# Three blocks of a transformer on one core: new order of the mixer heads, norms on four columns, divided weight tiles in the attention slots

## What is computed

```python
for i in range(2):
    x = x + 0.5 * swiglu(rmsnorm(x), w_gate, w_up, w_down)
    h = rmsnorm(x) @ w_in
    y_mla  = attention(rmsnorm(h_q) @ w_qb, rmsnorm(h_kv) @ w_kvb, rope(h_kpe))   # 8 heads
    y_conv = silu(layernorm(depthwise_conv31(a * sigmoid(g))))                   # 31 taps, 256 channels
    y_hy   = x2 * longconv(x1 * longconv(v))                                     # two rounds, in frequencies
    x = x + concat(rmsnorm(y_mla), rmsnorm(y_conv), rmsnorm(y_hy)) @ w_out
    x = x + 0.5 * swiglu(rmsnorm(x), ...)
x = rmsnorm(x)
proj = rmsnorm(x) @ w_in_2            # state-space branch, and 3 groups of windowed attention, 4 heads each
x = x + (gate_a * ssm(proj) @ w1 + gate_b * attention(proj) @ w2) @ w3
x = x + swiglu(rmsnorm(x), ...)
out = rmsnorm(x)
```

## Time and profile before

| what | us |
|---|---|
| median of 3 runs (lowest, highest) | 3437.59 (3435.35, 3446.17) |
| device time of the profiled execution | 3437.45 |
| its span, first to last instruction | 3435.6 |
| PE busy in it | 3296.0 |
| DVE, ACT, POOL busy | 1797.7, 750.0, 1831.1 |
| mean granted TensorE clock, as a share of full speed | 0.989 |

### The profile page before, as it was taken

How to read it: one execution, slowest core, us unless ns; L and a number is a source line. 1 busy time by engine, 2 the same in 40 slices (tenths; PEclk the granted TensorE clock), 3 DMA queues, 4 the chain that set the end, 5 groups by cost and what they waited for, 6 DMA issues and landing times.

```text
span 3435.6 us, 43891 instructions
## 1 busy us (share of the span) xinstructions
PE 3296.0 (96%) x14456; PEld 2576.4 (75%) x14456; DVE 1797.7 (52%) x1995; ACT 750.0 (22%) x1265; POOL 1831.1 (53%) x1026
## 2 busy tenths in 40 slices
PE   6999999989999999999989999999999999999997
PEld 5888875468887788876457888787777777878885
DVE  6642168663312753138755331476768886753313
ACT  2110115522211111013532220111122322222201
POOL 4556651056666646663026666554455555666664
PEclk9999999999999999999999999999999999999998
DMA  4223230023233322231002323322121222223232
GB/s 138 80 80 98 92 105 19 8 79 96 94 97 97 111 74 86 93 110 61 13 31 92 97 93 97 108 79 68 61 90 62 74 70 72 92 92 98 93 96 73
DMA packets 77141, 280.98 MB, mean 82 GB/s; under 512 B 9350, under 2 KB 9734, under 8 KB 76360
## 3 DMA queue, kind: packets, MB, share of 16 engines
q1 hardware_dynamic: 74016, 268.84, 24.3%
q10 hardware_dynamic: 2984, 10.27, 0.9%
HBM read 276.97 MB, written 2.10 MB: 81 GB/s over the span
## 4 chain that ended last, share of the span: by engine, by line
PE 83%; DVE 11%; issue 3%; ACT 2%; DVEq 0%; ACTq 0%; DMA 0%; SPq 0%
PE bank L499 25%; PE bank L504 24%; PE bank L503 24%; DVE x_lo L1638 1%; PE bank L716 1%; PE bank L780 1%; PE bank L634 1%; PE bank L798 1%; PE bank L704 1%; DVE scaled L1990 1%; DVE square_sum L1648 1%; DVE xbc L2155 0%; DVE y L1878 0%; PE bank L611 0%; PE bank L619 0%
## 5 line engine op out<-in xcount | busy, mean ns | idle before, releaser
L445 POOL TENSOR_SCALAR w_hi<-raw 128x1024 fp32r<-128x1024 f32 x504 | 550.7, 1093 | 1525.1 <-PE bank L499 1518.0
L448 POOL TENSOR_TENSOR w_lo<-raw,w_hi 128x1024 fp32r<-128x1024 f32 x504 | 1267.6, 2515 | 42.1
L499 PE MATMUL bank<-x_hi,w_hi 128*128 128x512 f32 x2896 | 1151.4, 398 | 56.2 <-DVE x_lo L1638 31.4
L504 PE MATMUL bank<-x_hi,w_lo 128*128 128x512 f32 x2896 | 1133.3, 391 | 0.0
L503 PE MATMUL bank<-x_lo,w_hi 128*128 128x512 f32 x2896 | 1132.9, 391 | 0.0
L499 PEld LDWEIGHTS bank<-x_hi,w_hi 128*128 128x128 f32 x2896 | 547.4, 189 | 193.9 <-issue 79.1
L503 PEld LDWEIGHTS bank<-x_lo,w_hi 128*128 128x128 f32 x2896 | 548.0, 189 | 116.2 <-issue 5.3
L504 PEld LDWEIGHTS bank<-x_hi,w_lo 128*128 128x128 f32 x2896 | 546.9, 189 | 116.4
L504 PE MATMUL bank<-hidden_hi,w_lo 128*128 (+1 forms) x880 | 347.6, 395 | 0.0
L499 PE MATMUL bank<-hidden_hi,w_hi 128*128 (+1 forms) x880 | 347.6, 395 | 0.0
L503 PE MATMUL bank<-hidden_lo,w_hi 128*128 (+1 forms) x880 | 347.6, 395 | 0.0
(11 more groups left out here) (372 smaller groups left out, 3260.4 us busy)
## 6 DMA issues: line engine op xcount, KB each, us to landing
raw<-in_w SPq DMA_DIRECT2D x504, 512.0 KB, 3.5
dft<-in_dft ACTq DMA_DIRECT2D x2, 1536.0 KB, 6.8
x<-in_x SPq DMA_DIRECT2D x2, 1024.0 KB, 6.8
out<-x SPq DMA_DIRECT2D x4, 512.0 KB, 2.6
mask<-in_mask ACTq DMA_DIRECT2D x1, 1536.0 KB, 7.1
filt_cos<-in_dft_filter ACTq DMA_DIRECT2D x2, 512.0 KB, 5.5
filt_sin<-in_dft_filter ACTq DMA_DIRECT2D x2, 512.0 KB, 7.3
sel<-in_sel ACTq DMA_DIRECT2D x1, 768.0 KB, 5.5
```

What stands on the lines that cost most here:

```text
L445: nc.gpsimd.tensor_scalar(w_hi[:, s % 2, :], raw[:, s, :], 1.0, 0.0, ALU.mult, ALU.add).then_inc(w_rounded, 1)
L448: nc.gpsimd.tensor_tensor(w_lo[:, s % 2, :], raw[:, s, :], w_hi[:, s % 2, :].bitcast(F32), ALU.subtract).then_inc(w_split, 1)
L499: first = nc.tensor.matmul(out, hi_w, hi, start=start, stop=False)
L504: return nc.tensor.matmul(out, lo_w, hi, start=False, stop=stop)
```

## The change

In the mixer's in-projection the two latent norms are made on four columns: four matmuls that put one column for each 128 tokens into the sum's bank, a root and a reciprocal of 128x4, and four matmuls that spread the columns over a bank again. The second sum and both spreads stand inside a tile, after 2 of its 8 chunks. Ten of the 62 taps, all of accumulator 0, move from the heads into the in-projection on VectorE. In the heads both `inverse` of the first round stand in head 2, the fillers are cut from 28 to 13 for each layer, the fourth score of head 3 comes after its last turn, ScalarE copies a turned tile ahead of the exponential of the same number in the second half of a head, and the first two exponentials of head 0 come ahead of the value copies, behind a small Exp on one column. `spectrum_terms` makes 6 operations instead of 8. In the second block the fourth tile is whole and the second sum behind it, and the waits for the joined norm stand in slot 0 before bank 2. In the slots the third tile beside is divided around the rounds r=2 and r=3; in slot 3 the tile that followed the slot is divided into four pieces and put into bank 0. The negation of the row maximum is made by the reduction itself, and `shift(2)` comes before the value tile. The last norm is made on four columns and the last `x_hi` and `x_lo` are left out, which nobody read. The core of the diff:

```diff
-            def in_projection(tiles, between):
+            def in_projection(tiles, inside, between):
 
                 for n in range(tiles):
                     pe.wait_ge(tile_free, c.next(tile_free))
-                    project(bank[RING[n % len(RING)]][:], arriving=2 if n == 0 else 0).then_inc(tile_ready, 1)
+                    to = bank[RING[n % len(RING)]][:]
+                    if n in inside:
+                        s = take()
+                        project_part(to, s, 0, 2)
+                        inside[n]()
+                        project_part(to, s, 2, DC).then_inc(tile_ready, 1)
+                    else:
+                        project(to, arriving=2 if n == 0 else 0).then_inc(tile_ready, 1)
...
-                    after(mixed_copied, 3)
...
                 for pair in range(2):
                     product(bank[KEY_BANKS[pair]][:], s, 4 + pair, latent_hi[2], latent_lo[2], True, True
                             ).then_inc(k_ready, 1)
+                if g:
+                    after(mixed_copied, 3)
                 query_tile(ROPE_BANKS[1], s, 6, rope_ready)
...
-                if h < 7:
+                if h < 7 and h != 3:
                     scores(h + 1, 3)
                 mix(h, 0)
                 turn(h, 2)
                 mix(h, 1)
                 turn(h, 3)
+                if h == 3:
+                    scores(h + 1, 3)
                 second_unit()
                 mix(h, 2)
-                run_idle({0: 4, 2: 2, 4: 4}.get(h, 0))
                 mix(h, 3)
...
+                def latent_sums(n):
                     if n == 2:
-
-                        after(norm_rms, 1)
+                        after(latent_scaled, 1)
                     after(norm_summed, n)
-                    nc.tensor.matmul(bank[SUM_BANK][:], ones[:], (square_sum[:] if n > 1 else square[:, 0, :]),
-                                     start=True, stop=True).then_inc(norm_sum, 1)
-
-                in_projection(IN_BLOCKS, {1: sum_squares, 4: lambda: latent_norm(1), 6: lambda: latent_norm(2)})
+                    for t in range(TT):
+                        last = nc.tensor.matmul(bank[SUM_BANK][:, t:t + 1],
+                                                (square_sum if n > 1 else square[:, 0])[:, t * P:(t + 1) * P],
+                                                ones[:, 0:1], start=True, stop=True)
+                    last.then_inc(norm_sum, 1)
+
+                def latent_spreads(n):
+                    after(latent_inverted, n)
+                    for t in range(TT):
+                        last = nc.tensor.matmul(bank[SUM_BANK][:, t * P:(t + 1) * P],
+                                                latent_root[:, t:t + 1].broadcast_to([P, P]), ident[:],
+                                                start=True, stop=True)
+                    last.then_inc(latent_spread, 1)
+
+                in_projection(IN_BLOCKS, {5: lambda: latent_spreads(1), 7: lambda: latent_sums(2),
+                                          8: lambda: latent_spreads(2)},
+                              {1: sum_squares, 4: lambda: latent_sums(1)})
+                after(latent_scaled, 2)
...
-                def first_inverse(o, n):
-                    run_idle(n)
-                    inverse(o, 0)
-
-                head(1, nothing, lambda: first_inverse(0, 5))
-                head(2, lambda: inverse(0, 1), nothing)
+                head(1, lambda: run_idle(1), nothing)
+                head(2, lambda: inverse(0, 0), lambda: inverse(0, 1))
                 head(3, lambda: signal_transposes(1), lambda: frequencies(1, 0))
                 head(4, lambda: frequencies(1, 1), nothing)
-                head(5, nothing, lambda: first_inverse(1, 4))
+
+                def first_inverse():
+                    run_idle(2)
+                    inverse(1, 0)
+
+                head(5, lambda: run_idle(1), first_inverse)
                 head(6, lambda: inverse(1, 1), conv_mean)
...
+                    if j == 0 and n == min(FIRST_SUM_BANKS):
+                        pe.wait_ge(both_means, 1)
+                        pe.wait_ge(rms_ready, 3 * LAYERS + 1)
...
+                def spread_tile(first, end):
+
+                    if first == 0:
+                        if more:
+                            pe.wait_ge(vt_ready, c.at(vt_ready) + 2)
+                        split_slot.append(take())
+                    last = project_part(bank[VALUE_TILE_BANK if more else LATE_TILE_BANK][:], split_slot[0], first, end)
+                    if end == DC:
+                        last.then_inc(tile_ready, 1)
+
+                split_slot = []
                 for r in range(RES):
+                    if r == 3 and not more:
+                        spread_tile(2, 4)
...
-                        beside(2)
+                        spread_tile(0, 6 if more else 2)
+                    elif r == 3:
+                        spread_tile(6 if more else 4, DC if more else 6)
...
+                if not more:
+                    spread_tile(6, DC)
...
-                s = take()
-                project_part(bank[VALUE_TILE_BANK][:], s, 0, 2)
+                project(bank[VALUE_TILE_BANK][:]).then_inc(tile_ready, 1)
                 sum_squares(FIRST_SUM_BANKS[1])
-                project_part(bank[VALUE_TILE_BANK][:], s, 2, DC).then_inc(tile_ready, 1)
-
-                pe.wait_ge(both_means, 1)
-                pe.wait_ge(rms_ready, 3 * LAYERS + 1)
                 for j in range(4):
                     attention_slot(j)
-                proj_tile()
...
+            pe.wait_ge(x_summed, c.next(x_summed, DC))
+            for t in range(TT):
+                last = nc.tensor.matmul(bank[SUM_BANK][:, t:t + 1], square_sum[:, t * P:(t + 1) * P], ones[:, 0:1],
+                                        start=True, stop=True)
+            last.then_inc(sum_ready, 1)
+            pe.wait_ge(root_inverted, c.next(root_inverted))
+            for t in range(TT):
+                last = nc.tensor.matmul(bank[SUM_BANK][:, t * P:(t + 1) * P],
+                                        final_root[:, t:t + 1].broadcast_to([P, P]), ident[:], start=True, stop=True)
+            last.then_inc(root_spread, 1)
...
+                        if g == 0:
+                            exponential(0, t)
...
-                        for t in range(3):
+                        for t in range(2):
                             exponential(h + 1, t)
                         turned(h, 2)
+                        exponential(h + 1, 2)
+                        turned(h, 3)
                         exponential(h + 1, 3)
-                        turned(h, 3)
                         return
...
                     for t in range(2, TT):
+                        turned(h, t)
                         exponential(h + 1, t)
-                        turned(h, t)
...
+                nc.scalar.activation(exp_warm[:], eps[:], ACT.Exp)
                 mla_inputs(0)
-                for t in range(TT):
+                for t in range(2, TT):
...
+                early = 10
+                tap_order = [(0, j) for j in range(early)]
+                for j in range(TAPS):
+                    tap_order.append((1, j))
+                    if early + j < TAPS:
+                        tap_order.append((0, early + j))
                 taken, tap_at = [0], [None, None]
...
+                latent_inverse()
+                gate_tiles()
+                latent_scale((2,), KV_NORM)
+                gate_product(0)
+                norm_squares(2, lambda: long_taps(2))
+                long_taps(2)
+                latent_inverse()
+                long_taps(3)
+                latent_scale((0, 1), Q_NORM)
+                dve.sem_inc(latent_ready, 1)
+                gate_tiles()
+                long_taps(3)
+                gate_product(1)
...
-                    nc.vector.tensor_tensor(first[0], re, f_re, ALU.mult)
-                    nc.vector.tensor_tensor(first[1], im, f_im, ALU.mult)
+                    nc.vector.tensor_tensor(products[:, 0:2, :].rearrange("p a n -> p (a n)"), low,
+                                            spectrum[:, k, o, :], ALU.mult)
                     nc.vector.tensor_tensor(first[2], re, f_im, ALU.mult)
                     nc.vector.tensor_tensor(first[3], im, f_re, ALU.mult)
                     (im, re), (f_re, f_im) = halves(high), halves(spectrum[:, 2 + k, o, :])
-                    nc.vector.tensor_tensor(second[0], im, f_re, ALU.mult)
-                    nc.vector.tensor_tensor(second[1], re, f_im, ALU.mult)
+                    nc.vector.tensor_tensor(key_rope[:], high, spectrum[:, 2 + k, o, :], ALU.mult)
...
-                    link(nc.vector.reduce_max(soft_max[:, r % 2:r % 2 + 1], w, AX_X))
-                    link(nc.vector.tensor_scalar(soft_shift[:, r % 2:r % 2 + 1], soft_max[:, r % 2:r % 2 + 1],
-                                                 -1.0, None, ALU.mult), soft_shifted)
```

(1 more changed line is left out.)

159 lines of the change are left out of this document (86 added, 73 removed).

## The result

| | us, median (lowest to highest) | ratio to before, 95% interval |
|---|---|---|
| before | 3440.98 (3435.35 to 3446.17) | |
| changed kernel | 3419.78 (3414.05 to 3422.53) | 0.9939, 0.9926 to 0.9952 |

The change is worth 21 us of the 44 that were forecast; 3419.78 lies outside the stated range of 3382 to 3413. The profiled execution of the changed kernel took 3421.57 us (span 3419.8), so that the two profiles differ by only 15.9 us. Ratios are set against runs of the kernel before on the same chip in the same session.

The account below looks back on a forecast made before the run. TensorE was taken as the main bound (83% of the chain, VectorE 11%), alternating with VectorE in the heads. 2 × (−2) + 2 × (−12.5) − 10.2 − 5.1 = −44.3 from 3437.45 gave 3393.1 us, range 3382 to 3413.

Parts of the forecast that it names:

- in-projection, both layers: Mixer's in-projection: wait of 1.90 and half clock 1.65 go, two spreads cost 1.62; about −2 us a layer.
- Heads 6 and 7 only shift: Last two heads of each mixer: they move in time without gain or loss, 0 us.
- I take no cost: In-projection: added waits for the spreads priced at 0, since a whole tile of 5.45 us lies between.
- The saving of 1.90: In-projection: TensorE's wait of 1.90 us before the second sum goes, as its input is ready by then.
- Rival (a): In-projection: early taps collide with GpSimd's splits, heads start 4 to 8 us late per layer; 3405 us, chance 0.12.
- two signs of failure: Forecast wrong if TensorE's head waits exceed 12.5 us, or its busy time falls 24 us and the span does not follow.
- Head 2's term: Head 2 to the next inputs: 21.2 us becomes TensorE's list of 18.2, with the inverse moved; −3.0 us a layer.
- The taps' term: Heads 4 and 5: seven fewer taps of 0.66 before `out_spectrum`, less 0.2 for taps in a row; −4.4 us a layer.
- ScalarE's order: Head 0: turned copy ahead of the exponential removes the mix's wait of 2.12 us; head's term −1.9.
- Rival (d): Heads: without fillers TensorE falls to 1.2 GHz and stays there, so the kernel is slower; 3465 us, chance 0.03.
- (b): Rival, heads: they give only half of their forecast, each engine having little slack; 3405 us, chance 0.16.
- (e): Rival: gains before head 6 and in the slots are given back at common waits; 3428 us, chance 0.04.

Follow-up runs that it names:

- the first experiment: Changed kernel with all 62 taps in the heads and none in the in-projection, against the changed kernel: 3424.95 us, ratio to before 0.9967.

## Why the prediction was wrong

The sum was −44.3; the profiled executions differ by −15.9. The 28.4 between, by the steps of the prediction:

| step | forecast | profiled | short by |
|---|---|---|---|
| in-projection, both layers | −4.0 | +8.6 | 12.6 |
| heads 0 to 5, both layers | −25.0 | −20.7 | 4.3 |
| "Heads 6 and 7 only shift" | 0 | +6.3 | 6.3 |
| second block | −10.2 | −12.8 | −2.6 |
| end | −5.1 | −3.7 | 1.4 |
| rest, untouched | 0 | +6.5 | 6.5 |

- **The in-projection failed at "I take no cost"**, the term for the added waits for the spreads. I had looked at TensorE's queue behind the added wait and found a whole tile of slack. The cost is on VectorE: the scaling waits there for the spread, and behind it in VectorE's queue stand the gated tile, six short tiles and then the remainder of the latents that TensorE needs first. The saving of 1.90 was itself too high by the 1.14 that is left: VectorE's product into `long_pad` took 1.34 us for 0.69 there, and its add of the squares 1.53 for 0.69, so that the sum's input, which was to be "ready by then", is late. Without any tap the wait is still 0.96, so the two taps ahead of it are not the reason. The spread in tile 7 gives back A to B of 87 to 89, between the forecast 85.3 and 90.
- **Rival (a) had the place and not the cause.** It priced a late start of the heads at 4 to 8 us a layer through taps held by splits. The splits do hold them (5.02 us for three), as the rule in the Trainium skill's page "SBUF — State Buffer", section "Who interferes with whom", has it; but of the wait of 3.35 only 0.7 goes with all the taps, and A to B stays at 90.7. I blamed the taps twice, in the rival and in the first experiment's theory.
- **Heads 0 to 5 were right in mechanism and nearly in size.** −10.3 a layer for −12.5. The prediction's two signs of failure do not decide it: TensorE's waits in the heads came to 12.9 and 11.4 us, on either side of the 12.5, and its busy time fell by 6.4 and not by 24. Head 2's term assumed that TensorE's list set the end; the last exponential behind `y_update` did, 2.28 us, and taking it away brings B to C to 62.7, 1.8 below the forecast's 64.5. The taps' term was −4.4, the experiment without them says 3.7 in the first layer and 2.1 in the second. ScalarE's order I valued at the 2.12 of one wait. It is worth 38 us in this kernel. I take it that with the fillers gone TensorE catches up with VectorE in every head, so that each late copy is waited for; this is argued, since no run has the old order with the fillers.
- **Heads 6 and 7 did not only shift.** The same new order made the last exponential of head 6 late, and I had followed it only in heads 0 to 3. The wait is 2.00 in every run with the new order in head 6, and 0.77 in those with the old. Its price is 1.2 us of wait and at times the lower clock: 2.4 and 3.9 us in the two layers.
- **Second block and end** held. The slots came to the forecast (−2.2 for −2.1 from one slot to the next), and the start to −5.3 for −4.3. But 1.5 of the −12.8 fell behind the slots, in code that the change leaves alone, and is luck. At the end the sum ran from 3405.54 to 3410.51; the matmuls at the lower clock and the handovers take 0.9 more than I gave them, and the last feed-forward part took 0.5 more.
- **Rival (d)** is out as a whole: the clock in the heads' window of the first layer is 0.99 (0.97 before). In the small it is in the numbers: in the changed kernel's mixers TensorE falls to 1.2 GHz behind some waits of 1.69 us and more, in one layer and not in the other.
- **Rivals (b) and (e).** The heads did not give half but four fifths, so (b) is out. (e) came nearest in the mixers, which kept 5.8 of 29 us, but through two losses with causes of their own and not at a common wait.
- **The rest** is the clock in untouched code. Nothing ties it to the change: the other kernels' profiles spread further there (last section).

The range was too narrow at its upper end because I let the two mixers' terms, each worked out once, count as known; a mistake in one of them counts twice.

## What to carry to other kernels

A wait that is moved to where its engine has slack must be priced on the engine that consumes its result too: list what stands behind the consumer in its queue, and who waits for the last of that. When fillers or slack are taken from one engine, an order on another engine that was worth two microseconds can decide the whole stretch; read it to the end of the last head, not to the first that gains. Where a kernel has two equal layers, cutting both traces at the same events and comparing segment by segment shows what the total hides.

## What the runs showed of the hardware

- TensorE's clock can drop in a stretch without any wait: here it did while it made 16 filter matmuls of one column each (granted 0.66 from 1210 to 1220 us, 1.00 before). The changed kernel's second layer, first feed-forward part, and then the same place before:

```profile
1212.08 2.62 PE L628 MATMUL bank<-ones,taps_abs 128*128 128x1 f32 x16
1214.56 0.77 PE L506 MATMUL bank<-x_hi,w_hi 128*128 128x512 f32 x1
```

```profile
1214.53 1.95 PE L619 MATMUL bank<-ones,taps_abs 128*128 128x1 f32 x16
1216.34 0.48 PE L499 MATMUL bank<-x_hi,w_hi 128*128 128x512 f32 x1
```

  The part from the first sum of squares to the one before the mixer, the same code in all kernels, took between 403.1 and 412.0 us in the first layer of the 14 profiled executions, and between 398.2 and 405.2 in the second.
- The same wait can be followed by either clock. The wait of 2.00 us before the squares of y was followed by four matmuls in 1.96 us in one layer and in 3.30 in the other. The inverse of head 2, 16 matmuls, took 5.30 us behind a wait of 1.69 in the first layer and 3.62 behind one of 1.48 in the second. So a wait's price here is its length, or its length plus some 1.3 to 1.7 us and in the inputs 2.8, and comparing one profile with another has this grain: three or four such drops are as much as the change was worth in the mixers (5.8 us in the profiles).
